# Encoder step with 32 experts: index masks ahead of the attention, a seventh slot for the weights, and 2 MB fetches at both ends of the expert loop

## What is computed

```
score = where(visible, sum_h w[h] * relu(q_idx[h] . k_idx), -inf); sel = top_k(score, 64 or 72)
probs = softmax(q . k[sel] / 8); att = probs @ v[sel]
h1  = LN1(2**0.25 * h + concat(att, pool) @ w_o)
out = 0
for e in range(32):                       # top 4 of 32 experts, others have gate 0
    gu  = h1 @ w1[e] + b1[e]              # w1[e]: 1024 x 2048, 8 MB
    act = (clip(up) + 1) * (min(gate, 7) * sigmoid(1.702 * gate))
    out += gates[:, e] * (act @ w2[e] + b2[e])   # w2[e]: 1024 x 1024, 4 MB
y   = LN2(2**0.25 * h1 + out)
```

## Time and profile before

| what | us |
|---|---|
| three timed executions | 1102.83, 1106.24, 1105.74 (median 1105.74) |
| profiled execution, its own time | 1103.82 |
| its span, first to last instruction | 1101.9 |
| PE busy | 1048.7 (95%) |
| DVE busy, ACT busy | 393.9, 238.7 |
| read from HBM | 420.11 MB |

### The profile page before, as it was taken

The page is one execution under the profiler, slowest core; times in us unless marked ns, Lnnn a source line. Parts: engine busy times, 40 slices in busy tenths (PEclk is TensorE's granted clock), DMA queues, the critical chain, the costliest instruction groups (busy, mean ns, idle before and its releaser), DMA issues.

```text
span 1101.9 us, 13984 instructions
## 1 busy us (share of the span) xinstructions
PE 1048.7 (95%) x5284; PEld 430.7 (39%) x5285; DVE 393.9 (36%) x697; ACT 238.7 (22%) x475; POOL 15.7 (1%) x29
## 2 busy tenths in 40 slices
PE   8989999999999999999999999999999999999996
PEld 7765453333333333333333333333333333333332
DVE  7873357322233222222233333323223223222226
ACT  3334113222221111222122222222112112212112
POOL 1003000000000000000000000000000000000000
PEclk9989899999999999999999999999999999999998
DMA  9750337999999999999999999999999999999992
GB/s 315 290 230 1 147 160 310 428 428 428 428 429 428 428 428 433 437 427 432 435 428 431 435 431 429 435 433 428 433 433 428 433 435 428 432 434 423 427 427 86
DMA packets 28556, 421.82 MB, mean 383 GB/s; under 512 B 5325, under 2 KB 5965, under 8 KB 11546
## 3 DMA queue, kind: packets, MB, share of 16 engines
q1 hardware_dynamic: 28346, 420.93, 90.4%
q10 hardware_dynamic: 192, 0.66, 0.2%
HBM read 420.11 MB, written 1.46 MB: 383 GB/s over the span
## 4 chain that ended last, share of the span: by engine, by line
PE 55%; DMA 34%; DVE 9%; issue 1%; ACT 1%; SPq 0%; DVEq 0%; ACTq 0%
DMA ring<-in_w_dram 34%; PE ps L928 29%; PE ps L954 10%; PE ps L646 4%; PE ps L773 3%; PE ps L991 2%; DVE area L1682 2%; PE ps L907 1%; DVE area L1660 1%; DVE area L1663 1%; DVE area L1656 1%; DVE area L1657 1%; PE ps L625 1%; PE ps L918 1%; DVE late L1442 1%
## 5 line engine op out<-in xcount | busy, mean ns | idle before, releaser
L928 PE MATMUL ps<-ring,area 128*64 128x512 f32 x1536 | 340.9, 594 | 15.9 <-DMA ring<-in_w_dram 15.9
L954 PE MATMUL ps<-ring,area 128*64 128x512 f32 x992 | 224.9, 595 | 0.0
L928 PEld LDWEIGHTS ps<-ring,area 128*64 128x64 f32 x1536 | 107.2, 137 | 225.9 <-issue 190.3
L1682 DVE TENSOR_TENSOR area<-area,ps 128x1024 f32<-128x1024 f32 (+1 forms) x96 | 116.5, 1214 | 55.5 <-PE ps L991 55.5
L1656 DVE TENSOR_SCALAR area<-ps 128x512 f32<-128x512 f32 x31 | 21.4, 692 | 272.2 <-PE ps L928 272.2
L928 PE MATMUL ps<-late,area 128*64 128x512 f32 x512 | 116.1, 595 | 0.0
L954 PEld LDWEIGHTS ps<-ring,area 128*64 128x64 f32 x992 | 67.5, 136 | 120.7 <-issue 118.3
L1289 ACT ACTIVATE area<-area 128x512 f32<-128x512 f32 x31 | 19.5, 629 | 404.4 <-DVE area L1656 404.4
L1648 DVE SCALAR_TENSOR_TENSOR y_sb<-ps,gcol,y_sb 64x512 fp32r<-64x512 f32 x62 | 46.5, 750 | 98.4 <-ACT y_sb L1250 98.0
L991 PE MATMUL ps<-y_sb,giveT 128*128 128x512 f32 x192 | 69.5, 444 | 11.8 <-DVE area L1682 11.8
L898 PE MATMUL ps<-area 128*64 128x512 bf16 x558 | 66.1, 382 | 0.0
(11 more groups left out here) (245 smaller groups left out, 663.5 us busy)
## 6 DMA issues: line engine op xcount, KB each, us to landing
ring<-in_w_dram SPq DMA_DIRECT2D x50, 4096.0 KB, 21.7
ring<-in_w_dram SPq DMA_DIRECT2D x60, 2048.0 KB, 16.4
late<-in_w_dram SPq DMA_DIRECT2D x10, 4096.0 KB, 26.7
late<-in_w_dram SPq DMA_DIRECT2D x12, 2048.0 KB, 15.2
area<-in_w_o_dram SPq DMA_DIRECT2D x1, 4096.0 KB, 14.1
area<-in_w_in_dram SPq DMA_DIRECT2D x1, 2560.0 KB, 16.7
area<-in_w_in_dram SPq DMA_DIRECT2D x1, 2336.0 KB, 9.4
area<-in_w_in_dram SPq DMA_DIRECT2D x1, 2048.0 KB, 20.7
```

The lines of the kernel that those rows point to most:

```text
L928: last = mm(ps_gu[g * BLK:(g + 1) * BLK, c, :], x[:, spot(k), :], half_of(w, c, g), start=False, stop=(k == KT - 1))
L954: last = mm(ps_y[g * BLK:(g + 1) * BLK, :], hT[:, c, h, :], w2_t[:, h, c, g * 512:(g + 1) * 512], start=False, stop=(h == 1 and c == 3))
L1682: v.tensor_tensor(acc, acc, src[0:n, :, :], ALU.add).then_inc(done, 1)
```

## The change

1. `home` holds `ring` and `area` in one piece, so that `ring` has a seventh slot, over the first 4096 columns of `area`. `out_acc` moves into `rows`. Slots 2 and 3 now hold `w2`; quarters 3 and 4 of `w1` stand in 4 and 5 in even passes, in 5 and 6 in odd ones. Quarter 4 of odd passes (`fourth_odd`) has its own semaphore, `w_in_last`, and is fetched a pass earlier; the first, for pass 1, goes out in the front.
2. Fetches are 2 MB for pairs 0 to 6 and for the last two pairs, 4 MB for pairs 7 to 12. Pairs 4 to 6 have an order of their own. `ln2` is fetched behind all weights, into slot 0.
3. In the front DVE computes the index scores of tile 2 and `mask_logits(0)` between the rounds for tile 1. PE projects block 9 after the index logits, and turns the reciprocals at the start of `attend`. The dummy products in `attend` give way to the first three heads of the next tile's logits or, for tile 2, to a part of `mix(1)`.
4. At the start of the loop PE turns the first tokens ahead of its read of the number of passes; the split of the rows into three bf16 parts and the start of the sums are interleaved on DVE.

The core of the diff:

```
-    WIDE_PAIR = 4
+    EVEN_HOME = (0, 1, 4, 5, 2, 3)
+    USE_PAIR = 4
+    WIDE_PAIR = 7
...
-        ring = sb("ring", [P, NSLOT, SLOT])
-        area = sb("area", [P, KT * IN])
+        home = sb("home", [P, NSLOT * SLOT + KT * IN])
+        ring = home[:, 0:(NSLOT + 1) * SLOT].rearrange("p (s n) -> p s n", s=NSLOT + 1)
+        area = home[:, NSLOT * SLOT:]
...
+        out_acc = rows
...
             sp.wait_ge(pv_ps, NT)
             sp.wait_ge(att_ready, NT)
             sp.wait_ge(rows_out, 16 * 11)
+            sp.dma_start(ring[:, NSLOT, :], w1_part(1, 3)).then_inc(w_in_last, 16)
...
-            with sp.Fori(0, WIDE_PAIR) as i:
-                in_order_of_release(i)
-            sp.wait_ge(split_ready, NT)
-            sp.dma_start(ln2[:, 0, :], ...)
-            sp.dma_start(ln2[:, 1, :], ...)
-            with sp.Fori(WIDE_PAIR, end_wide) as i:
-                in_order_of_use(i, True)
-            in_order_of_use(end_wide, False)
+            with sp.Fori(0, USE_PAIR) as i:
+                even = expert_of(sp, 2 * i + 2)
+                first_half(i, even, False, False)
+                third_even(2 * i + 2, even)
+                odd = expert_of(sp, 2 * i + 1)
+                third_odd(2 * i + 1, odd)
+                down(2 * i + 1, odd, False)
+                after = expert_of(sp, 2 * i + 3)
+                first_half(i, after, True, False)
+                fourth_even(2 * i + 2, even)
+                fourth_odd(2 * i + 3, after)
+                down(2 * i + 2, even, False)
+            with sp.Fori(USE_PAIR, WIDE_PAIR) as i:
+                first_half(i, even, False, False)
+                third_odd(2 * i + 1, odd)
+                down(2 * i + 1, odd, False)
+                third_even(2 * i + 2, even)
+                fourth_even(2 * i + 2, even)
+                first_half(i, after, True, False)
+                fourth_odd(2 * i + 3, after)
+                down(2 * i + 2, even, False)
+            third_odd(2 * WIDE_PAIR + 1, expert_of(sp, 2 * WIDE_PAIR + 1))
+            with sp.Fori(WIDE_PAIR, end_wide) as i:
+                down(2 * i + 1, expert_of(sp, 2 * i + 1), True)
...
+            down(2 * end_wide + 5, expert_of(sp, 2 * end_wide + 5), False)
+            sp.wait_ge(slot_free[0], end_wide + 3)
+            sp.dma_start(ln2[:, 0, :], ...)
+            sp.dma_start(ln2[:, 1, :], ...)
...
                 pe.wait_ge(exp_done, t + 1)
                 if t >= 1:
                     pe.wait_ge(att_ready, t)
+                pe.wait_ge(inv_ready, t + 1)
+                tr(ps[0:N_HEADS, 3, 0:n], row_inv[0:n, t, :], ident[0:n, 0:n]).then_inc(invT_ps, 1)
...
-                keep_warm(3, bank=2)
+                if t < 2:
+                    logits_of(t + 1, range(3))
+                else:
+                    mix(1, pool_ks, True, False)
                 pe.wait_ge(probsT_sb, pe_groups[0])
-                pe.wait_ge(inv_ready, t + 1)
-                tr(ps[0:N_HEADS, 7, 0:n], row_inv[0:n, t, :], ident[0:n, 0:n]).then_inc(invT_ps, 1)
...
-            for t in range(2):
-                hide_late_keys(t)
-                keep_top(t)
-            for i in range(8, 12):
-                index_scores(i)
-            mask_logits(0)
-            keep_top(2)
+            hide_late_keys(0)
+            top_rounds(0, topk[0] // 8)
+            hide_rest(0)
+            index_scores(8)
+            index_scores(9)
+            hide_late_keys(1)
+            top_rounds(1, topk[1] // 32)
+            index_scores(10)
+            index_scores(11)
+            top_rounds(1, topk[1] // 32)
             mask_logits(0)
+            top_rounds(1, topk[1] // 8 - topk[1] // 32 * 2)
+            hide_rest(1)
+            top_rounds(2, topk[2] // 8)
+            hide_rest(2)
             inverse(0)
```

More of the change, by code:

```diff
@@ new lines, in fourth_odd, with third_even, fourth_even, second_half_wide @@
+            def fourth_odd(p, e):
+                fourth(p - 1, e, NSLOT, slot_free[3], w_in_last)
+            def third_even(p, e):
+                third(p - 1, e, 4, slot_free[2])
+            def fourth_even(p, e):
+                fourth(p, e, 5, slot_free[2], w_in_slot[3])
+            def second_half_wide(p, e, odd):
+                sp.wait_ge(slot_free[3] if odd else slot_free[2], p)
+                sp.dma_start(ring[:, 5:7, :] if odd else ring[:, 4:6, :],
+                             w1_v[col(e), 1].rearrange("e p n -> p (e n)"))\
+                    .then_inc(w_in_slot[3] if odd else w_in_slot[2], 16)
@@ new lines, in down @@
+            def down(p, e, wide):
+                if wide:
+                    sp.wait_ge(slot_free[4], p)
+                    sp.wait_ge(slot_free[5], p)
+                    sp.dma_start(ring[:, 2:4, :], w2_whole[col(e)].rearrange("e p n -> p (e n)"))\
+                        .then_inc(w_in_slot[4], 16)
+                    return
+                for h in range(2):
+                    sp.wait_ge(slot_free[4 + h], p)
+                    sp.dma_start(ring[:, 2 + h, :], w2_v[col(e), h].rearrange("e p n -> p (e n)"))\
+                        .then_inc(w_in_slot[4 + h], 16)
@@ new lines, in _ @@
+            third_odd(2 * WIDE_PAIR + 1, expert_of(sp, 2 * WIDE_PAIR + 1))
+            with sp.Fori(WIDE_PAIR, end_wide) as i:
+                down(2 * i + 1, expert_of(sp, 2 * i + 1), True)
+                even = expert_of(sp, 2 * i + 2)
+                first_half(i, even, False, True)
+                second_half_wide(2 * i + 2, even, False)
+                down(2 * i + 2, even, True)
+                after = expert_of(sp, 2 * i + 3)
+                first_half(i, after, True, True)
+                second_half_wide(2 * i + 3, after, True)
@@ new lines, in _ @@
+            with sp.Fori(end_wide, end_wide + 2) as i:
+                down(2 * i + 1, expert_of(sp, 2 * i + 1), False)
+                even = expert_of(sp, 2 * i + 2)
+                first_half(i, even, False, False)
+                third_even(2 * i + 2, even)
+                fourth_even(2 * i + 2, even)
+                down(2 * i + 2, even, False)
+                after = expert_of(sp, 2 * i + 3)
+                first_half(i, after, True, False)
+                third_odd(2 * i + 3, after)
+                fourth_odd(2 * i + 3, after)
@@ L781, in _ @@
             attend(0)
-            logits_of(1)
+            logits_of(1, range(3, N_HEADS))
             project(12)
@@ L792, in _ @@
             attend(1)
-            logits_of(2)
+            logits_of(2, range(3, N_HEADS))
             pe.wait_ge(proj_sb, len(order))
@@ L1263, in _ @@
                 act.wait_ge(part_rest, t + 1)
-                copy(rows_b[:, t, 1, :], rows[:, t, :]).then_inc(part_mid, 1)
+                copy(rows_b[:, t, 1, :], (flat, flat_too, flat)[t]).then_inc(part_mid, 1)
             end = last_pass(act)
@@ L1433, in scale_rows, with top_rounds, hide_rest @@
                 v.tensor_tensor(rows[0:n, t, :], rows[0:n, t, :], lnb[0:n, 1, :], ALU.add).then_inc(ln_done, 1)
-            def keep_top(t):
+            def top_rounds(t, n_rounds):
+                _, n, nk = tiles[t]
+                sc = score[0:n, t, 0:nk]
+                for _ in range(n_rounds):
+                    link(v.max(max8[0:n, t, :], sc))
+                    link(v.match_replace(sc, max8[0:n, t, :], sc, TAKEN))
+            def hide_rest(t):
                 _, n, nk = tiles[t]
@@ L1602, in _ @@
             dve.wait_ge(const_ready, 9)
-            link(v.tensor_scalar(passes[:, 2 * MAXP:2 * MAXP + 1], half, float(NE // 2 - 2) - ROUND, None, ALU.add))
+            link(v.tensor_scalar(passes[:, 2 * MAXP:2 * MAXP + 1], half, float(NE // 2 - 3) - ROUND, None, ALU.add))
             begun = earlier_of[:, 0:NE - 1]
```

231 lines of the change are left out of this document (128 added, 103 removed).

## The result

| kernel | median of runs | lowest to highest | mean granted clock |
|---|---|---|---|
| before, 20 runs | 1104.66 us | 1100.96 to 1106.83 | 0.991 (profiled execution) |
| changed, 20 runs | 1107.44 us | 1103.36 to 1109.52 | 0.988 |

The ratio is 1.0025, 95% interval 1.0016 to 1.0034: the change makes the kernel slower by a quarter of a per cent, where a gain of 2 us was forecast. The profiled execution of the changed kernel took 1103.36 us (span 1100.8, clock 0.991) and is the quickest of its 20.

What follows compares the result with a forecast made beforehand. The memory stream was taken to bound the kernel from the loop's first fetch. Loop -3.1 plus front +1.1 gave -2.0 us, from the mean 1104.7 to 1102.7; likeliest case 1100 to 1106, eight in ten 1098 to 1108.5.

Steps and rivals of the forecast that it cites:

- Steps 1 to 3 of the front: Front: logits start at about 62.9, projections take 8.0, reciprocal comes at about 79.5, so PE stands 6 us.
- Step 2: Front, two projections behind tile 0's logits: without the earlier waits they take 8.0 us, not 9.95; PE reaches `attend(0)` at 73.7.
- Step 4: Front, behind PE's stand: low clock adds 2.0 us, next projections begin at 89.4, not 85.60: +3.8, or +1.8 if clock holds.
- The slow rival: Wait for the reciprocal lowers the clock into projections 12 and 13 and the mix: front +6, seams +4, 1109.6 us; chance 0.14.
- Step 6: Front, `attend(2)` and following mix: dummy products go and low clock may go: -1.9 us, bounds -3.2 and +0.4.
- Step 7: End of the front: PE's read of the pass count runs beside ACT's copy of the first tokens: -0.7 us.
- The seventh slot: Loop: quarter 4 of pass 1 is fetched in the front while DMA idles, so the stream has one slot less: -4.9 us.
- `ln2`, -2.4: Loop: fetching `ln2` behind all weights takes 1.05 MB out of the stream: -2.4 us.
- 2 MB fetches, +2.2: Loop: four more pairs in 2 MB fetches, 8 passes at 428 in place of 432 GB/s: +2.2 us.
- Seams, +2: Loop: at pair 7's seam SP issues nothing for about 13 us and the queue may run dry: +2 us, bounds 0 and 8.
- (a), (b), (d) and (e): Signs: reciprocals turned near 79.7 after 6 us wait; clock full, then low; 428 and 432 GB/s; last landing about 900 us.
- (c): Sign, end of the front: the first up product comes about 1 us later than in the kernel before.

Runs made afterwards that it cites:

- the trace with dummy products: Changed kernel with 22 dummy products on PE ahead of the wait for the first reciprocal: 1103.42 us, ratio to before 0.9995.
- the two best: Changed kernel, pair 7 written out, reciprocal of tile 0 before tile 2's rounds, two rounds moved later: 1095.14 us; second adds four dummy products in two attend parts: 1093.81.
- the one attempt: Changed kernel with pair 7 written out, first half of pass 16 fetched ahead of pass 15's `w2`: 1106.67 us, ratio to before 1.0020.

## Why the prediction was wrong

The direction failed in the front. The sum was -3.1 in the loop and +1.1 in the front; in its place stand -2.2 and +4.7.

- **Steps 1 to 3 of the front: right.** The logits start within 0.3 us of the forecast, the reciprocal at 79.88 (forecast 79.5), PE stands 6.66 us (forecast 6) with the named work queued behind.
- **Step 2: right, but not in each execution.** The projections took 8.03 in the first trace and 9.72 in the second, although the waits ahead of them (0.49 and 0.29) are the same. In six of nine traces with this order the clock is 1.00 from 64 to 72 us, in three 0.79; in the five with the old order it is 0.57 to 0.79.
- **Step 4: the step that failed**, and it failed in size. It forecast the start of the next projections at 89.4; they start at 90.75, 93.01, 92.87 and 93.02 in four traces with this front, mean 92.4, and at 85.60, 84.82, 84.80 and 84.77 in four with that of before, mean 85.0: +7.4 us for the forecast +3.8. It said that the clock would be low behind the stand, and the edit that keeps most of the clock is worth 4.0 to 4.4 us by the medians. Three of its terms were too small. (1) The 2.0 for small products: from the turned reciprocals to the end of the values went 5.9 us in the first trace and 8.0 in the other three, where 6.7 was forecast and 4.3 is what the trace with dummy products shows. (2) The 3.0 for the five remaining logits: 4.6 in all four (86.16 to 90.75 in the first), of which 1.36 is a wait for DVE, which first multiplies by the reciprocals (0.69) and masks the first heads; with the dummy products it is still 4.1, so most of this miss is not the clock. (3) Nothing for the 32 projections behind, taken at 8.03; they took 9.58, 9.91, 9.00 and 9.17, 1.0 to 1.9 us more. The text had the earlier trace rows for this, where a shorter wait slowed 32 projections by 1.9 us; it took that back as a gain in step 2 and did not pay it again in step 4. The slow rival names exactly this ("it stays down into projections 12 and 13") and got a chance of 0.14.
- **Step 6: right in mechanism, too small in size.** The clock is 1.00 from 124 to 140 us in eight of the nine traces (7.13 a mix), and 0.79 with the old order. The ninth is the second trace shown, in which one mix takes 8.83. From the second mix to the last, 30.4 us in four traces of before are 26.1 in three with this front and 27.8 in the second one: -4.3 and -2.6 for the forecast -1.9, whose lower bound was -3.2.
- **Step 7, the start of the loop, -0.7: right, a little large.** From the start of the last mix to the first up product it is 25.71 to 25.81 us in the four traces with the old start (146.16 to 171.87), and 25.18 in the seven with the new start and the changed front, the two best apart (148.32 to 173.50): -0.5. The two best have 24.83. The kernel with the old front and the new start has 26.59 there and its first up product at 173.02, but also a granted clock of 0.94 from 140 to 170 us, where all other traces have 1.00; why the clock fell in that trace is open.
- **The front in sum.** The first up product comes at 173.50, 177.81, 176.48 and 176.15 in four traces with this front, mean 176.0, and at 171.87, 171.13, 171.18 and 170.98 in four with that of before, mean 171.3: +4.7 for +1.1. Step 4 makes +7.4 of it, and all behind it makes -2.7, just what steps 5 to 7 were to give. That is luck in part: the unpaid projections and the larger gain of step 6 balance. The upper bound of +6 is added up nowhere in the text; its steps reach 3.8 - 0.1 + 0.4 - 0.7 = +3.4. The loop's stretch goes from 907.5 to 905.3: -2.2 for -3.1. With 0.5 us outside the span (below) that is +3.0; the medians show +2.8 to +3.0.
- **The seventh slot, -4.9:** a gain, of 2.7 us by the medians and of 4.6 against the traces with a like dent. Only the first figure speaks against the forecast.
- **`ln2`, -2.4: not shown for the changed kernel.** In the kernel before its move alone gives nothing that the medians can tell, since it filled a gap. The step took all bytes ahead of the last fetch for equal; there they were not. In the changed loop that gap is not seen, and the forecast's own terms with the dent as measured, -4.9 - 2.4 + 2.2 + 2.4 = -2.7, are what the first trace shows (904.4 against 907.1). With nothing for `ln2` and 2.7 for the slot the sum would be +1.9.
- **2 MB fetches, +2.2: right as far as is seen.** The windows have 428 for 432 GB/s, and the stretches +2.3 with one trace of the edit, 0.1 us for each of the 24 additional fetches. The Trainium skill (DMA: Bandwidth & Descriptors, Anatomy of one DMA — SWDGE (gpsimd) path) gives the fixed cost of about 2.0 us for DMAs that GpSimd issues; here SP issues them. The estimate of 48 us worked out from it does not hold here, where fetches are queued ahead: the medians moved by 1.2.
- **Seams, +2: a little low.** SP's two issues there are 13.3 us apart (583.82 and 597.14 in the first trace), as forecast. The dent at pair 7 costs 2.4 to 4.8 us in six traces, by the rate from 560 to 620 us: in its lowest window of 10 us the rate is 292, 315 and 318 GB/s where the stretch is 904.0 to 904.4 us, and 229, 223 and 252 where it is 906.4. So most of what two executions differ by in the loop is this one gap.
- **Small slips of the working.** The passes "29.1 us apart" are 28.94 in the rows beside it; 29.1 is worked out from 432 GB/s. The front of +6.4 at which the slow rival decides is counted from 1105.74, the forecast from 1104.7; from there it would be +7.4. Neither moves the forecast.

Of the signs named in advance, (a), (b), (d) and (e) came true in the first trace: 80.22 behind 6.66 us, the clock full ahead of the stand and low behind it, 428 and 431 GB/s, 1077.91 - 177.30 = 900.6 us from the loop's first fetch to the last landing, tail 22.9. (c) was +1.6 there and +4.7 as a mean. A reader who had only that trace would call the prediction right.

The deeper fault was to size a clock term from one execution. The Trainium skill (TensorE: Matmul & The Clock Gate, Part 1: The HAM clock gate (the "warmup" mystery)) says of the cold products at a kernel's start that their number varies between runs of the same kernel, and that their penalty is under 1% of a typical span. Behind a stand in mid-kernel both agree with the runs (10.4 and 16.9 us at the lower level in two executions; the 4.4 us of the dummy products' edit are 0.4% of 1107), but 0.4% is more than this whole change moved.

Open stay: why the changed kernel spends about 0.5 us more outside its span (2.5 and 2.4 us in its two sets of runs, 2.4 to 2.8 in all kernels with the changed loop, and 1.9 in before, in `ln2` last and in the one with more 2 MB pairs), and whether a seam can be built without a gap at all, which the one attempt did not do.

## What to carry to other kernels

When an edit makes PE stand, price two things apart: the wait itself, and the low clock on everything dense behind it; here the second was some 4 us, and all else in the front was almost balanced. Follow the queue of the engine that PE waits for down to the single instruction: a reciprocal of 0.20 us, nine rounds too late, turned a gain of 5 to 6 us into a loss of 3. And before a fetch is moved out of a stream, look whether the place that it leaves has anything else to move: in the kernel before, the stream was the bound, and 1 MB in one of its gaps still cost nothing.

## What the hardware showed unexpectedly

- The same instructions with the same waits got 10.4 us of low clock behind the stand in one execution and 14.8 to 16.9 us in three (granted clock 0.71, 0.53, 0.57 and 0.59 from 80 to 98 us). The quickest of 20 runs was 4.1 us under their median.
- 22 dummy products, 5.07 us of PE, with 1.65 us of standing behind them, were enough to keep the clock at its upper level for most of what followed.
- The last fetch took 22.00 us from issue to landing where `ln2` was queued right behind it, and 21.18 and 21.58 where nothing was, in two kernels that differ in this alone. The second has two traces and the first only one, and the ten traces with the changed loop, where `ln2` is last too, have 21.98 to 22.84.
